# Attention of the even mixer regrouped from 32 steps of one head to 16 steps of two, and a small buffer padded

## The chip, the cores and the metric

The kernel runs on one core of a Trainium2 chip. The metric is the device time of one execution in microseconds; the time of a kernel is the median of its runs. A run that is profiled also leaves a trace of every instruction. TensorE (PE, with its weight loads as PEld), VectorE (DVE), ScalarE (ACT), GpSimd (POOL) and SyncE (SP) each work through a program of their own and meet at semaphores.

## What is computed

Two layers over 256 latent and 256 context tokens of width 1024, in float32. Each layer is a half-step FFN, a token mixer, a half-step FFN. The change lies in the mixer of the even layer, whose attention part is:

```python
s_band = jnp.einsum("bnqkgd,bnjkd->bkgnqj", qb, kb).astype(jnp.float32) * scale   # latent keys, |i-j| <= 128
s_ctx = jnp.einsum("bnqkgd,bckd->bkgnqc", qb, kc).astype(jnp.float32) * scale     # all context keys
p = jax.nn.softmax(jnp.concatenate([s_band, s_ctx, sink_logits(sink, s_band.shape)], axis=-1), axis=-1)
o = p[latent] @ v + p[context] @ vc
```

There are 8 query heads of 64 channels and 2 key heads. Latent queries see 512 keys, context queries the 256 context keys. A learned value per head, the sink, joins the softmax's sum. Beside the attention the same mixer has a convolution of 31 taps over 512 channels, and the adaLN parameters of later sub-layers (`silu(c) @ mod_w`) are computed while it runs.

## The kernel before, in words

**Order of the work.** Each engine has a hand-written program in one block. An FFN is a loop over "units": a unit's weights (up to 1 MB) come by DMA into `raw`, ACT rounds them into `w_hi` (L805), DVE makes the rest `w_lo` (L1083), and PE does three products per tile (`three`, L396 to L398): hi by hi, hi by lo, lo by hi. The up projection reads `hn_hi` and `hn_lo` as the moving operand, the down projection `a_hi` and `a_lo` (12 or 10 tiles of 512 tokens per unit, 8 units per half FFN). The last FFN has 256 tokens only.

**The even mixer** goes through 7 input units. PE does the first five whole; the two gate and value units of the convolution's last two channel groups are cut into 16 pieces (`conv_step`, six matmuls each), of which four go before the attention and 12 into it.

**The attention before.** `ATT` lists 32 steps (pair of heads tt, stream s, head of the pair h2, half of the queries qt). s = 0 is latent (512 keys), s = 1 context (256 keys). One step j goes through:
- PE `scores` (L570): the 128 queries by the keys, 64 channels deep, into bank 4 + j % 2. Head h2 sits on partitions 64·h2 to 64·h2 + 63, so on its own half of the array's rows. A float32 product is two passes, "x2" in the rows.
- DVE `largest`: mask and maximum (L1309) for s = 0, maximum (L1312) for s = 1, then the shift (L1314).
- ACT `expo`: the exponential with its sum (L926) and the sink's (L928).
- DVE `denominator` (L1321, L1322), ACT `normalise` (L934).
- PE `turn` (L579): 4 or 2 transposes into bank 6 + j % 2; ACT `turned` (L941) copies them to `pT`.
- PE `values` (L596): the product with V, 64 columns wide, in two halves spread over two steps; the group of four steps of one (tt, s) fills half of the partitions with each head. ACT `att_head` (L947) and DVE (L1333) then make `hn_hi` and `hn_lo` of it.

**The engines' loops** run one step after another, staggered: in round j PE issues `scores(j+1)`, conv pieces, `turn(j-1)`, `values` of an earlier step, and from round 10 on one quarter of an adaLN job (`mod_products`, L432: 8 products on 32 columns each, sixteen passes). DVE in round j does `largest(j)`, `denominator(j-1)`, the group's rest, and some taps of the convolution (`taps`, L1266, one tap for 128 channels and 512 tokens). ACT does `expo(j)`, `normalise(j-1)`, `turned(j-2)`. In rounds 4 and 9 ACT also makes a sigmoid (L961, its own table) and rounds a unit (L805), and DVE waits for the sigmoid (`gated_value`, L1252). All queues are in order.

**The adaLN jobs** 6 to 11 have 24 quarters of 1 MB each. `mod_raw` holds four; POOL issues the load (L388) of the next job's quarter as soon as PE has used the present one. After a job's four quarters ACT copies the row (`mod_rows`, L838), PE spreads it (`mod_columns`, L441, with `sel` as moving operand), DVE adds the bias (`mod_vector`, L1172). The first quarter of a job waits for the row of the job before.

**After the attention** PE sums the convolution's output over channels (L626), the layer norm follows (L1351 and others), and the output projection starts with the attention's half, then the convolution's.

**Memory.** On-chip buffers lie one behind the other in the order of their declaration, each rounded up to 32 bytes. `hn_hi` starts at byte 32896 of a partition (a multiple of 128). `sel` takes 32 bytes; behind it come `shared`, `c_act`, `modT`, then `a_hi`, `a_lo`, `mod_raw`, and in the same room the mixers' own buffers. `a_hi` starts at 146720, which is 32 past a multiple of 128. Weights (`w_hi`, `w_lo`) lie ahead of `sel`, on multiples of 128.

Of the kernel before, what the change touches and what calls it, by code (L numbers as in the profile page):

```python
# [84 lines left out]
def build(nc, t, out):  # L85
# [3 lines left out]
    with ExitStack() as ctx:  # L89
# [24 lines left out]
        sel = sb("sel", [P, 8])  # L114
# [90 lines left out]
        s_mm = sem("s_mm")  # L205
        max_made = sem("max_made")
# [65 lines left out]
        def att_slot(j):  # L272

            i = j - ATT_FROM
            return ATT_JOBS[0] + i // 4, i % 4
# [116 lines left out]
        def _(pe):  # L392
# [171 lines left out]
            def scores(j):  # L564
                tt, s, h2, qt = ATT[j]
                if j >= 2:
                    pe.wait_ge(exp_made, j - 1)
                k0 = LAT * s
                a = LAT * s + qt * P
                pe.matmul(ps[:, 4 + j % 2, k0:KEYS], qk[64 * h2:64 * h2 + 64, tt, a:a + P],  # L570
                          qk[64 * h2:64 * h2 + 64, CT, k0:KEYS], start=True, stop=True).then_inc(s_mm, 1)

            def turn(j):
                tt, s, h2, qt = ATT[j]
                pe.wait_ge(p_made, j + 1)
                if j >= 2:
                    pe.wait_ge(pT_made, j - 1)
                for kt in range(2 * s, 4):
                    last = pe.transpose(ps[:, 6 + j % 2, kt * P:(kt + 1) * P], prod[:, j % 2, kt * P:(kt + 1) * P],  # L579
                                        ident)  # L580
                last.then_inc(pT_mm, 1)

            def values(j, half):

                tt, s, h2, qt = ATT[j]
                g = j // 4
                kts = range(2 * s, 4)
                kts = kts[:len(kts) // 2] if half == 0 else kts[len(kts) // 2:]
                if half == 0:
                    pe.wait_ge(pT_made, j + 1)  # L590
                    if g >= 2:
                        pe.wait_ge(mix_made, g - 1)
                    if g == 0:
                        pe.wait_ge(unit_evac, E + 5)
                for kt in kts:
                    last = pe.matmul(ps[64 * h2:64 * h2 + 64, g % 2, 0:LAT], v_att[:, kt, 64 * h2:64 * h2 + 64],  # L596
                                     pT[:, (j // 2) % 2, kt, :], start=(kt == 2 * s), stop=(kt == 3))
                if half == 1:
                    last.then_inc(pv_mm, 1)

            NJ = len(ATT)
            scores(0)
            for j in range(NJ + 3):
                if j + 1 < NJ:
                    scores(j + 1)
                if j < 4:
                    conv_step(2, 4 + j)
                if 5 <= j < 9:
                    conv_step(3, 2 * j - 10)
                    conv_step(3, 2 * j - 9)  # L610
                if 1 <= j < NJ + 1:
                    turn(j - 1)
                if j >= 3:
                    values(j - 2 - (j + 1) % 2, (j + 1) % 2)
                if ATT_FROM <= j < ATT_FROM + 4 * len(ATT_JOBS):
                    m, q = att_slot(j)
                    mod_products(m, q, q + 1)
                    if q == 1 and m > ATT_JOBS[0]:
                        mod_columns(m - 1)
            mod_columns(ATT_JOBS[-1])  # L620
# [169 lines left out]
        def _(act):  # L790
# [128 lines left out]
            def expo(j):  # L919
                tt, s, h2, qt = ATT[j]  # L920
                act.wait_ge(max_made, j + 1)
                if j >= 2:
                    act.wait_ge(pT_mm, j - 1)
                src = ps[:, 4 + j % 2, LAT:KEYS] if s else gact[:, j % 2, :]
                neg = att_cols[:, 1, j:j + 1]
                act.activation(prod[:, j % 2, LAT * s:KEYS], src, ACT.Exp, bias=neg, scale=HD ** -0.5,  # L926
                               accum_out=att_cols[:, 2, j:j + 1])
                act.activation(att_cols[:, 3, j:j + 1], col("sink", tt + 4 * h2), ACT.Exp, bias=neg).then_inc(exp_made, 1)  # L928

            def normalise(j):  # L930
                tt, s, h2, qt = ATT[j]
                act.wait_ge(den_made, j + 1)
                p = prod[:, j % 2, LAT * s:KEYS]
                act.activation(p, p, ACT.Copy, scale=att_cols[:, 5, j:j + 1]).then_inc(p_made, 1)  # L934

            def turned(j):
                tt, s, h2, qt = ATT[j]
                act.wait_ge(pT_mm, j + 1)
                if j // 2 >= 2:
                    act.wait_ge(pv_mm, j // 2 - 1)  # L940
                act.activation(pT[:, (j // 2) % 2, 2 * s:4, qt * P:(qt + 1) * P],  # L941
                               ps[:, 6 + j % 2, 2 * s * P:4 * P].rearrange("p (k q) -> p k q", q=P),
                               ACT.Copy).then_inc(pT_made, 1)
# [767 lines left out]
```

## Time and profile before

| what | value |
|---|---|
| median of 3 runs | 1949.94 us (1946.14 to 1950.98) |
| the profiled execution's own time | 1950.95 us |
| its span | 1949.2 us |
| mean granted TensorE clock | 0.971 |
| PE / PEld / DVE / ACT busy | 95% / 77% / 46% / 32% |

The span is 1.75 us shorter than the execution's own time, which is 1.0 us above the median. PE is busy in nearly all of it. The attention stands between 508 and 641 us.

### The profile page before, as it was taken

What the parts mean: (1) busy time and instruction counts of PE and PEld (TensorE: products, weight loads), DVE (VectorE), ACT (ScalarE), POOL (GpSimd) and SP (SyncE); (2) the same over time, 40 slices, a digit from 0 to 9 for tenths busy, and PEclk for the clock granted to TensorE, in tenths of its full rate; (3) what the DMA queues carried; (4) which work ended last, traced back from release to release, by engine and by line L of the source; (5) the groups of instructions that cost most, each with busy time, mean ns of one, the idle gap of its engine ahead of it and who ended that gap; (6) DMA issues with size and microseconds to landing.
All of it is one profiled execution on the core that took longest, in us unless ns stands there. A gap on an engine that the chain in (4) does not pass through costs nothing.

```text
span 1949.2 us, 25181 instructions
## 1 busy us (share of the span) xinstructions
PE 1844.9 (95%) x10094; PEld 1491.5 (77%) x10094; DVE 887.5 (46%) x1375; ACT 614.6 (32%) x824; POOL 36.3 (2%) x72
## 2 busy tenths in 40 slices
PE   3999999999889999999999999999998998899996
PEld 1788778868544668888888688888877988589996
DVE  2433323345878552333334533333344455865555
ACT  2322122233445332212222322222223133244342
POOL 0000000000001000000000000000000000000000
PEclk7999999999899989999999999999998999999998
DMA  8522452243148353222213422232232224045553
GB/s 337 218 86 87 173 194 86 75 164 124 44 163 306 137 193 131 82 96 103 106 64 111 169 90 92 81 108 108 68 126 111 87 88 151 1 176 186 179 178 103
DMA packets 39108, 252.39 MB, mean 129 GB/s; under 512 B 4465, under 2 KB 5873, under 8 KB 14449
## 3 DMA queue, kind: packets, MB, share of 16 engines
q1 hardware_dynamic: 29232, 179.91, 26.3%
q0 software_dynamic: 9792, 71.31, 9.5%
q8 instruction: 61, 1.00, 0.2%
q14 instruction: 23, 0.18, 0.0%
HBM read 250.15 MB, written 1.05 MB: 129 GB/s over the span
## 4 chain that ended last, share of the span: by engine, by line
PE 87%; DVE 7%; ACT 2%; DMA 2%; issue 2%; SPq 0%; ACTq 0%; DVEq 0%
PE ps L396 26%; PE ps L398 26%; PE ps L397 26%; PE ps L432 3%; PE ps L596 1%; DMA xT<-in_xT 1%; DVE w_lo L1083 1%; DVE y L1266 1%; PE ps L570 1%; PE ps L743 1%; ACT w_hi L805 1%; PE ps L456 1%; PE ps L579 1%; DVE t_ring L1144 1%; PE ps L710 0%
## 5 line engine op out<-in xcount | busy, mean ns | idle before, releaser
L396 PE MATMUL ps<-hn_hi,w_hi 128*128 128x512 f32 (+2 forms) x1784 | 646.3, 362 | 12.4 <-DVE hn_lo L1160 8.2
L397 PE MATMUL ps<-hn_lo,w_hi 128*128 128x512 f32 (+2 forms) x1784 | 640.4, 359 | 0.0
L398 PE MATMUL ps<-hn_hi,w_lo 128*128 128x512 f32 (+2 forms) x1784 | 640.1, 359 | 0.0
L1083 DVE TENSOR_TENSOR w_lo<-raw,w_hi 128x2048 fp32r<-128x2048 f32 (+2 forms) x184 | 377.0, 2049 | 569.7 <-ACT w_hi L805 569.6
L805 ACT ACTIVATE w_hi<-raw 128x2048 fp32r<-128x2048 f32 (+2 forms) x184 | 316.6, 1721 | 823.5 <-PE ps L398 814.2
L396 PEld LDWEIGHTS ps<-hn_hi,w_hi 128*128 128x128 f32 (+1 forms) x1784 | 338.8, 190 | 77.3 <-issue 24.4
L398 PEld LDWEIGHTS ps<-hn_hi,w_lo 128*128 128x128 f32 (+1 forms) x1784 | 338.9, 190 | 50.5 <-issue 0.3
L397 PEld LDWEIGHTS ps<-hn_lo,w_hi 128*128 128x128 f32 (+1 forms) x1784 | 339.1, 190 | 48.4 <-issue 0.7
L396 PE MATMUL ps<-a_hi,w_hi 128*128 128x512 f32 (+1 forms) x704 | 258.9, 368 | 1.8 <-DVE a_lo L1198 1.8
L398 PE MATMUL ps<-a_hi,w_lo 128*128 128x512 f32 (+1 forms) x704 | 258.5, 367 | 0.0
L397 PE MATMUL ps<-a_lo,w_hi 128*128 128x512 f32 (+1 forms) x704 | 258.5, 367 | 0.0
L1101 DVE SCALAR_TENSOR_TENSOR xT<-ps,modT,xT 128x256 f32 (+1 forms) x136 | 59.9, 479 | 235.3 <-PE ps L398 235.3
L396 PEld LDWEIGHTS ps<-a_hi,w_hi 128*128 128x128 f32 x704 | 132.5, 188 | 26.8 <-DVE a_lo L1198 2.2
L398 PEld LDWEIGHTS ps<-a_hi,w_lo 128*128 128x128 f32 x704 | 132.5, 188 | 24.2
L397 PEld LDWEIGHTS ps<-a_lo,w_hi 128*128 128x128 f32 x704 | 132.5, 188 | 24.1
L863 ACT ACTIVATE a_hi<-prod 128x512 f32 (+3 forms) x88 | 50.9, 578 | 212.3 <-DVE prod L1195 212.3
L432 PE MATMUL ps<-mod_raw,c_act 128*32 128x256 f32 x1152 | 84.6, 430 | 17.5 <-DMA mod_raw<-in_mod_w 13.8
L1198 DVE TENSOR_TENSOR a_lo<-prod,a_hi 128x512 f32 (+3 forms) x88 | 55.1, 626 | 71.7 <-ACT a_hi L863 71.7
L432 PEld LDWEIGHTS ps<-mod_raw,c_act 128*32 128x32 f32 x1152 | 34.8, 119 | 62.0 <-issue 36.7
L1266 DVE SCALAR_TENSOR_TENSOR y<-upad,cols,y 128x512 f32<-128x512 f32 x120 | 82.0, 743 | 0.0
L396 PE MATMUL ps<-w_hi,hn_hi 128*128 128x256 f32 x256 | 76.1, 297 | 4.9 <-DVE shared L1394 4.9
L397 PE MATMUL ps<-w_lo,hn_hi 128*128 128x256 f32 x256 | 73.7, 288 | 0.0
(181 smaller groups left out, 1182.6 us busy)
## 6 DMA issues: line engine op xcount, KB each, us to landing
raw<-in_w_up SPq DMA_DIRECT2D x88, 1024.0 KB, 4.9
mod_raw<-in_mod_w POOLq DMA_DIRECT2D x68, 1024.0 KB, 7.1
raw<-in_w_downA SPq DMA_DIRECT2D x32, 768.0 KB, 4.3
raw<-in_w_downB SPq DMA_DIRECT2D x32, 640.0 KB, 3.9
raw<-in_w_od_in SPq DMA_DIRECT2D x16, 1024.0 KB, 4.8
raw<-in_w_ev_in SPq DMA_DIRECT2D x7, 1024.0 KB, 4.9
mod_raw<-in_mod_w SPq DMA_DIRECT2D x4, 1024.0 KB, 11.0
raw<-in_w_ev_out SPq DMA_DIRECT2D x4, 1024.0 KB, 4.9
```

The source lines that it names most:

```text
L396: pe.matmul(o, lh, rh, start=first, stop=False)
L397: pe.matmul(o, lh, rl, start=False, stop=False)
L398: return pe.matmul(o, ll, rh, start=False, stop=last)
L432: last = pe.matmul(ps[32 * g:32 * g + 32, product_bank(m), 0:LAT], c_act[:, k, :], mod_raw[:, k, g * LAT:(g + 1) * LAT], start=(k == 0), s ...
L456: pe.matmul(ps[:, 7, 0:W[n]], ones, rstd[:, 0:W[n]], start=True, stop=True).then_inc(rstd_mm, 1)
L570: pe.matmul(ps[:, 4 + j % 2, k0:KEYS], qk[64 * h2:64 * h2 + 64, tt, a:a + P], qk[64 * h2:64 * h2 + 64, CT, k0:KEYS], start=True, stop=True ...
L805: act.activation(w_hi[:, u0 % 2, 0:n], raw[:, u0 % 2, 0:n], ACT.Copy).then_inc(hi_made, 1)
L863: act.activation(a_hi[:, j + 2 * r, 0:w], prod[:, j, 0:w], ACT.Copy).then_inc(a_hi_made, 1)
L1083: dve.tensor_tensor(w_lo[:, u0 % 2, 0:n], raw[:, u0 % 2, 0:n], w_hi[:, u0 % 2, 0:n], ALU.subtract).then_inc(lo_made, 1)
L1101: last = dve.scalar_tensor_tensor(out=xT[:, d0 + 2 * r, tokens(s)], in0=ps[:, bank(u0, b), tokens(s)], scalar=modT[:, vec, d0 + 2 * r, s:s ...
L1198: dve.tensor_tensor(a_lo[:, j + 2 * r, 0:w], prod[:, j, 0:w], a_hi[:, j + 2 * r, 0:w], ALU.subtract).then_inc(a_made, 1)
L1266: ins = dve.scalar_tensor_tensor(out=dst, in0=src, scalar=col("conv_w", i * CT + c), in1=dst, op0=ALU.mult, op1=ALU.add)
```

## The change

There are 16 steps now: `ATT` is (tt, qt, s), and a step holds both heads of a pair. The stream s alternates from step to step. The two heads' score products are issued one behind the other: for s = 0 into banks 4 and 5, for s = 1 into the two halves of bank 1, where the second waits for the first (`s_half`) and a conv piece or an adaLN quarter stands between. Transposes go to banks 6 and 7, one for each head. The value products of both heads alternate, all into bank 0. DVE and ACT handle two heads per operation where they can. The conv pieces stand in rounds 0 to 8 (`CONV_AT`), two adaLN quarters go into each of the rounds 10 to 21, and the loops run to round 22 or 23. `sel` is padded to 32 floats.

```diff
-        sel = sb("sel", [P, 8])
+        sel = sb("sel", [P, 32])[:, 0:8]
-            pT = sb("pT", [P, 2, 4, LAT], F32, s)
+            pT_full = sb("pT_full", [P, 2, 4, LAT], F32, s)
+            pT_ctx = sb("pT_ctx", [P, 2, 2, LAT], F32, s)
+        def att_quarters(j):
+            at = [2 * (j - ATT_FROM) + i for i in range(2)]
+            return [(ATT_JOBS[0] + i // 4, i % 4) for i in at if 0 <= i < 4 * len(ATT_JOBS)]
+        def att_rows(j):
+            return [m for i, m in enumerate(ATT_JOBS) if j == ATT_FROM + 2 * i + 2]
+        CONV_AT = {0: ((2, 4), (2, 5)), 1: ((2, 6),), 2: ((2, 7),), 4: ((3, 0),), 5: ((3, 1), (3, 2)),
+                   6: ((3, 3), (3, 4)), 7: ((3, 5), (3, 6)), 8: ((3, 7),)}
+        GATED_AT = {3: 2, 9: 3}
-        EARLY = 28
+        EARLY = 30
         def taps_by(j):
             if j < 9:
-                return EARLY + (TAPS - EARLY) * (j + 1 if j < 4 else j) // 8
-            return min(2 * TAPS, TAPS + TAPS * (j - 9) // 24)
+                return EARLY + (TAPS - EARLY) * (j + 1) // 9
+            return min(2 * TAPS, TAPS + TAPS * (j - 8) // 12)
-        ATT = [(tt, s, h2, qt) for tt in range(4) for s in range(2) for h2 in range(2) for qt in range(2)]
+        ATT = [(tt, s, qt) for tt in range(4) for qt in range(2) for s in range(2)]
@@ PE
+            def score(j, h2):
+                tt, s, qt = ATT[j]
+                if h2 == 0 and j >= 2:
+                    pe.wait_ge(exp_made, j - 1)
+                if h2 == 1 and s == 1:
+                    pe.wait_ge(s_half, j // 2 + 1)
...
+                last = pe.matmul(score_place(s)[:, h2, :], qk[64 * h2:64 * h2 + 64, tt, a:a + P],
+                                 qk[64 * h2:64 * h2 + 64, CT, LAT * s:KEYS], start=True, stop=True)
+            def values(tt, s):
+                g = 2 * tt + s
+                pe.wait_ge(pT_made, 4 * tt + 2 + s + 1)
+                if g >= 1:
+                    pe.wait_ge(mix_made, g)
...
+                for i, kt in enumerate(att_keys(s)):
+                    for h2 in range(2):
+                        last = pe.matmul(ps[64 * h2:64 * h2 + 64, 0, 0:LAT], v_att[:, kt, 64 * h2:64 * h2 + 64],
+                                         turned_place(s)[:, h2, i, :], start=(i == 0), stop=(kt == 3))
+            for j in range(NJ + 7):
+                between = [(conv_step, a) for a in CONV_AT.get(j, ())]
+                between += [(mod_products, (m, q, q + 1)) for m, q in att_quarters(j)]
                 if j + 1 < NJ:
-                    scores(j + 1)
+                    score(j + 1, 0)
+                    if ATT[j + 1][1] == 1:
+                        step, a = between.pop(0)
+                        step(*a)
+                    score(j + 1, 1)
+                for step, a in between:
+                    step(*a)
                 if 1 <= j < NJ + 1:
                     turn(j - 1)
+                if j >= 5 and (j - 5) % 4 < 2 and j < NJ + 3:
+                    values((j - 5) // 4, (j - 5) % 4)
+                for m in att_rows(j):
+                    mod_columns(m)
@@ ACT
+                for h2 in range(2):
+                    i = 2 * j + h2
+                    src = gact[:, h2, :] if s == 0 else score_place(s)[:, h2, :]
+                    act.activation(weight_place(s)[:, h2, :], src, ACT.Exp, bias=att_cols[:, 1, i:i + 1],
+                                   scale=HD ** -0.5, accum_out=att_cols[:, 2, i:i + 1])
...
+                act.activation(turned_place(s)[:, :, :, qt * P:(qt + 1) * P],
+                               ps[:, 6:8, 0:n * P].rearrange("p h (k q) -> p h k q", q=P), ACT.Copy).then_inc(pT_made, 1)
+                if j in GATED_AT:
...
+                if j >= 6 and (j - 6) % 4 < 2 and j < NJ + 4:
+                    att_head(2 * ((j - 6) // 4) + (j - 6) % 4)
@@ DVE
                 if s == 0:
+                    for h2 in range(2):
+                        last = dve.tensor_tensor_reduce(out=gact[:, h2, :], in0=score_place(s)[:, h2, :],
+                                                        in1=att_mask[:, qt, :], scale=1.0, scalar=-3e38, op0=ALU.add,
+                                                        op1=ALU.max, accum_out=top[:, h2:h2 + 1])
                 else:
+                    link(dve.reduce_max(top, score_place(s), AX.X))
+                dve.scalar_tensor_tensor(out=att_cols[:, 1, 2 * j:2 * j + 2], in0=top, scalar=-HD ** -0.5, in1=sinks,
+                                         op0=ALU.mult, op1=ALU.min).then_inc(max_made, 1)
-                if j >= 7 and (j - 3) % 4 == 0:
+                if j >= 7 and (j - 7) % 4 < 2 and j < NJ + 5:
+                    g = 2 * ((j - 7) // 4) + (j - 7) % 4
-                if j in (11, 13):
-                    rest_of(E + 7 + (j - 11) // 2)
+                if j in (10, 11):
+                    rest_of(E + 7 + j - 10)
+                for m in att_rows(j - 1):
+                    mod_vector(m)
```

## Rows read from the trace of the kernel before

**Rows 1.** The page: busy time of the engines, share of the span, instructions.
```profile
PE 1844.9 (95%) x10094; PEld 1491.5 (77%) x10094; DVE 887.5 (46%) x1375; ACT 614.6 (32%) x824; POOL 36.3 (2%) x72
```
**Rows 2.** Chain that ended last, 400 to 1000 us: start, us, what.
```profile
509.12 2.65 DVE y L1266 x4
...
560.91 2.20 DVE w_lo L1083
...
641.29 3.54 PE ps L626 x8
```
**Rows 3.** Busy time by stretch; last three: granted clock, DMA share, GB/s.
```profile
526.00:534.00 8.00, 7.93 (x22) 5.07 (x21) 5.74 (x15) 6.77 (x10) 0.00 (x0) 0.57 0.00 0
571.00:641.00 70.00, 65.51 (x519) 29.61 (x515) 56.28 (x147) 35.49 (x105) 11.64 (x22) 1.00 0.91 316
```
**Rows 4.** Waits, 507 to 645 us: total, times, longest.
```profile
DVE hn_lo L1333 <- ACT hn_hi L947: 12.1, 8, 3.7
...
DVE upad L1252 <- ACT t_ring L961: 7.4, 2, 3.9
```
**Rows 5.** PE in order of time: start, us, instructions with their count.
```profile
586.34 0.65 PE L596 MATMUL ps<-pT,v_att 128*64 128x256 f32 x2
586.91 1.07 PE L432 MATMUL ps<-mod_raw,c_act 128*32 128x256 f32 x16
587.91 1.12 PE L570 MATMUL ps<-qk 64*128 64x512 f32 x2
588.97 0.66 PE L579 MATMUL ps<-mats,prod 128*128 128x128 f32 x4
...
596.92 1.08 PE L596 MATMUL ps<-pT,v_att 128*64 128x256 f32 x4
...
598.93 0.70 PE L570 MATMUL ps<-qk 64*128 64x256 f32 x2
```
**Rows 6.** DVE in order of time: an s = 0 round, then an s = 1 round.
```profile
515.45 0.68 DVE L1309 CUSTOM_DVE_ANT_0 gact<-ps,att_mask 128x512 f32<-128x512 f32 x1
...
516.57 2.72 DVE L1266 SCALAR_TENSOR_TENSOR y<-upad,cols,y 128x512 f32<-128x512 f32 x4
...
532.21 0.42 DVE L1312 TENSOR_REDUCE att_cols<-ps 128x1 f32<-128x256 f32 x1
...
533.06 2.72 DVE L1266 SCALAR_TENSOR_TENSOR y<-upad,cols,y 128x512 f32<-128x512 f32 x4
```
**Rows 7.** ACT in order of time, round 4 with its sigmoid.
```profile
524.98 0.71 ACT L934 ACTIVATE prod<-prod,att_cols 128x512 f32<-128x512 f32 x1
525.59 0.58 ACT L941 ACTIVATE pT<-ps 128x512 f32<-128x512 f32 x1
526.19 1.28 ACT L961 ACT_TABLE_LOAD   x1
527.49 0.60 ACT L961 ACTIVATE t_ring<-ps 128x512 f32<-128x512 f32 x1
...
531.20 0.48 ACT L926 ACTIVATE prod<-ps,att_cols 128x256 f32<-128x256 f32 x1
```
**Rows 8.** Landing times of `mod_raw` 440 to 650 us; two stretches of the DMA.
```profile
DMA to landing us min/median/max: 5.0/5.3/8.0
...
435.00:445.00 10.00, 8.87 (x40) 6.05 (x40) 9.21 (x23) 5.50 (x13) 0.53 (x1) 0.67 1.01 425
636.00:640.00 4.00, 3.93 (x40) 1.41 (x38) 2.11 (x5) 0.41 (x2) 1.09 (x3) 1.00 0.94 360
```
**Rows 9.** Matmul groups of the first FFN (60 to 425 us), then of the last.
```profile
L397 PE MATMUL ps<-hn_lo,w_hi 128*128 128x512 f32 x339 | 131.9, 389 | 0.0
L397 PE MATMUL ps<-a_lo,w_hi 128*128 128x512 f32 x174 | 69.0, 396 | 0.0
...
L397 PE MATMUL ps<-hn_lo,w_hi 128*128 128x256 f32 x416 | 118.0, 284 | 0.0
L397 PE MATMUL ps<-a_lo,w_hi 128*128 128x256 f32 x176 | 49.2, 280 | 0.0
```

More of the change, by code:

```diff
@@ L562, in _ @@
             pe.wait_ge(v_made, 1)
-            def scores(j):
-                tt, s, h2, qt = ATT[j]
-                if j >= 2:
+            def score(j, h2):
+                tt, s, qt = ATT[j]
+                if h2 == 0 and j >= 2:
                     pe.wait_ge(exp_made, j - 1)
-                k0 = LAT * s
+                if h2 == 1 and s == 1:
+                    pe.wait_ge(s_half, j // 2 + 1)
                 a = LAT * s + qt * P
-                pe.matmul(ps[:, 4 + j % 2, k0:KEYS], qk[64 * h2:64 * h2 + 64, tt, a:a + P],
-                          qk[64 * h2:64 * h2 + 64, CT, k0:KEYS], start=True, stop=True).then_inc(s_mm, 1)
+                last = pe.matmul(score_place(s)[:, h2, :], qk[64 * h2:64 * h2 + 64, tt, a:a + P],
+                                 qk[64 * h2:64 * h2 + 64, CT, LAT * s:KEYS], start=True, stop=True)
+                if h2 == 1:
+                    last.then_inc(s_mm, 1)
+                elif s == 1:
+                    last.then_inc(s_half, 1)
@@ L573, in turn @@
             def turn(j):
-                tt, s, h2, qt = ATT[j]
+                tt, s, qt = ATT[j]
                 pe.wait_ge(p_made, j + 1)
[L576 to L580, printed above, removed]
-                last.then_inc(pT_mm, 1)
[L583 to L599, printed above, removed]
@@ L601, in _ @@
-            NJ = len(ATT)
-            scores(0)
-            for j in range(NJ + 3):
-                if j + 1 < NJ:
-                    scores(j + 1)
[L606 to L610, printed above, removed]
+                if j >= 1:
+                    pe.wait_ge(pT_made, j)
+                for h2 in range(2):
+                    for i in range(len(att_keys(s))):
+                        last = pe.transpose(ps[:, 6 + h2, i * P:(i + 1) * P],
+                                            weight_place(s)[:, h2, i * P:(i + 1) * P], ident)
@@ new lines, in turn @@
+                last.then_inc(pT_mm, 1)
+            def values(tt, s):
[3 more added lines that the diff above has]
+                    pe.wait_ge(mix_made, g)
+                else:
+                    pe.wait_ge(unit_evac, E + 5)
+                for i, kt in enumerate(att_keys(s)):
+                    for h2 in range(2):
+                        last = pe.matmul(ps[64 * h2:64 * h2 + 64, 0, 0:LAT], v_att[:, kt, 64 * h2:64 * h2 + 64],
+                                         turned_place(s)[:, h2, i, :], start=(i == 0), stop=(kt == 3))
+                last.then_inc(pv_mm, 1)
@@ L930, in normalise @@
+                for h2 in range(2):
+                    i = 2 * j + h2
+                    last = act.activation(att_cols[:, 3, i:i + 1], col("sink", tt + 4 * h2), ACT.Exp,
+                                          bias=att_cols[:, 1, i:i + 1])
+                last.then_inc(exp_made, 1)
             def normalise(j):
-                tt, s, h2, qt = ATT[j]
+                tt, s, qt = ATT[j]
                 act.wait_ge(den_made, j + 1)
-                p = prod[:, j % 2, LAT * s:KEYS]
-                act.activation(p, p, ACT.Copy, scale=att_cols[:, 5, j:j + 1]).then_inc(p_made, 1)
+                for h2 in range(2):
+                    p = weight_place(s)[:, h2, :]
+                    last = act.activation(p, p, ACT.Copy, scale=att_cols[:, 5, 2 * j + h2:2 * j + h2 + 1])
@@ L936, in turned @@
+                last.then_inc(p_made, 1)
             def turned(j):
-                tt, s, h2, qt = ATT[j]
+                tt, s, qt = ATT[j]
+                n = len(att_keys(s))
                 act.wait_ge(pT_mm, j + 1)
[L939 to L943, printed above, removed]
+                if tt >= 1 and qt == 0:
+                    act.wait_ge(pv_mm, 2 * (tt - 1) + s + 1)
@@ L945, in att_head @@
+                act.activation(turned_place(s)[:, :, :, qt * P:(qt + 1) * P],
+                               ps[:, 6:8, 0:n * P].rearrange("p h (k q) -> p h k q", q=P), ACT.Copy).then_inc(pT_made, 1)
             def att_head(g):
[L946 to L947 removed]
+                act.wait_ge(pv_mm, g + 1)
+                act.activation(hn_hi[:, CT + g // 2, tokens(g % 2)], ps[:, 0, 0:LAT], ACT.Copy).then_inc(att_hi, 1)
@@ L949, in _ @@
             NJ = len(ATT)
-            for j in range(NJ + 3):
+            for j in range(NJ + 7):
+                for m in att_rows(j):
+                    mod_rows(m)
                 if j < NJ:
@@ L956, in _ @@
                     turned(j - 2)
-                if j in (4, 9):
-                    c = 2 if j == 4 else 3
+                if j in GATED_AT:
+                    c = GATED_AT[j]
                     act.wait_ge(unit_mm, E + 4 + c)
```

66 lines of the change are left out of this document (24 added, 42 removed).

## The prediction, made before the changed kernel was run

> **What bounds the kernel now.** I began with the page: PE is busy for 95% of the span [rows 1], and the FFNs around the mixer keep it so. Where a stage lasts as long as PE's instructions, only fewer or shorter PE instructions help. Next the chain of waits: in the attention it first runs through DVE's taps, then through PE, and at 641.29 it enters the sum for the layer norm [rows 2]. DVE's first softmax part ends in taps at 509.12, so the stage runs from 508 to 641.3, some 133 us. The busy time by stretch shows two halves. From 571 to 641 PE is busy for 65.5 of 70 us at the full clock, and the DMA engines for 91% [rows 3]. Before that the engines wait for each other, and the clock was granted at 0.57 in one stretch, that is, mostly at 1.2 instead of 2.4 GHz [rows 3]. The waits tell for what: DVE stood 7.4 us before the two sigmoids and 12.1 us before the eight head outputs [rows 4].
>
> **PE's terms.** Taken at the full clock, start to start (a row's length less some 0.07 that it overlaps the next) [rows 5]: a 512-key score 1.06 us (two passes of about 0.43 and 0.2 of filling after another shape), a 256-key score 0.63; four transposes 0.59 (0.11 each and 0.15 per call; one pass of 128 columns is half of a 256-column pass); two value passes 0.57, four 1.00 (0.22 each, 0.15 per call); an adaLN quarter 1.00.
> Do two products side by side share their time? The quarter shows it: its sixteen passes of 256 columns take 1.00 us, four take 1.00 us in the value products [rows 5]. Four column strips ran at once. I take this for two column halves (values) and, less surely, for two row halves (scores); no row shows the latter. Bounds for a pair of 512-key scores: 1.1 (together) to 1.9 (in turn); I take 1.1.
> - Scores: before 16·1.06 + 16·0.63 = 27; after 8·1.1 + 16·0.63 = 19, as the 256-key ones stay apart. Minus 8, at worst minus 1.
> - Values: 96 passes in 32 calls were 16·1.00 + 16·0.57 = 25; after, 96·0.22/2 + 8·0.15 = 12. Minus 13, at worst minus 3.
> - Transposes: same 96, half the calls: minus 16·0.15 = 2.4.
> - Conv pieces, quarters and `mod_columns` stay.
> PE had some 112 us of work at the full clock and keeps about 88. It will no longer be the bound, so these 24 us are not the gain.
>
> **DVE's terms.** An s = 0 round takes 1.12 us before its taps (515.45 to 516.57), an s = 1 round 0.85 (532.21 to 533.06) [rows 6]; a tap 0.66 (four in 2.65 [rows 2]). A two-head round repeats the 0.61 mask operation and its reading of the sum: 1.8 us. With s = 1 the maximum covers 512 instead of 256 numbers, plus 0.27: 1.12 us. So 16·(1.12 + 0.85) = 31.5 becomes 8·(1.8 + 1.12) = 23.4.
>
> **ACT's stall.** DVE waits for each sigmoid, behind what ACT has queued. In the new rounds 3 and 9 (both s = 1) these are two exponentials (0.36 + 0.10 each) and two sink terms (0.18 each), 1.3; normalising two 512-wide heads, 1.24; a 512-wide copy, 0.58 (round 3: two heads of 256); the table 1.28 and the sigmoid 0.6 [rows 7]. Together 5.0, less 0.2 of DVE work beside it: 4.8, twice, where the two took 7.4 before [rows 4]. PE runs dry there too, its clock falls, and it catches up at half speed while DVE still has taps; I count that at nothing as long as DVE is behind.
>
> **Sum of the stage.** DVE from round 0 to the end of round 15: 68 taps, 44.6; softmax parts, 23.4; five head outputs, 1.7; two units' rests of 2.2 [rows 2], 4.4; the two gated values, 1.2; two `mod_vector`, 0.3; stalls, 9.6. That is 85.2 us, so round 16 begins at 508.2 + 85.2 = 593.4. PE in these rounds has 37 + 33 = 70, ACT some 60. The 12.1 us before head outputs shrink to little: each output now has a whole round between its steps. Bound: 0 to 12; I take 0, with the range for the rest.
> From round 16 on there is no softmax. DVE has 26 taps and little else, 19 us. But 12 quarters are left, two per round, and the DMA has to bring eight of them after their room is freed: the first is asked for at 1.6 us into round 16, lands after 5.3 us (median [rows 8]), and seven follow at the rate of a full queue, 425 GB/s, 1.049 MB in 2.47 us [rows 8]. The last lands at 593.4 + 1.6 + 5.3 + 17.3 = 617.6. Its products, row and columns add 2.1: 619.7. The PE idles in this tail, and I add 2 us for some of it and of the layer norm's sum at 1.2 GHz (bounds 0 and 6). The norm's sum then starts at 621.5 instead of 641.3: **minus 19.8 us**. What follows is unchanged.
>
> **The padding.** `sel` grows from 32 to 128 bytes, so all behind it moves by 96, and `a_hi` from 32 past a multiple of 128 to a multiple of 128. Does PE read it faster? In the first FFN a 512-wide matmul with `a_lo` moving takes 396 ns, with `hn_lo`, which lies on such a multiple, 389 [rows 9]. Weights, clock and width are the same. The other difference is that the down projection adds into one bank without alternating; but with 256 tokens, where that would hurt more, `a_lo` is the faster one, 280 against 284 [rows 9]. This leaves the address as the likelier cause, though why only the long stream would pay for it no row tells. The 512-wide down projections have 3·8·22·3 = 1584 such matmuls, back to back and on the chain. At 7 ns each: **minus 11.1 us**. Bounds: plus 2 (the 528 short ones lose their 4 ns) and minus 16 (it falls to the short ones' overhead, 10 ns less). The mixer's buffers move too; no row prices that, nothing is taken.
>
> **Total.** 1950.95 − 19.8 − 11.1 = 1920.1 for an execution like the profiled one; the median was 1.0 lower, so **1919**.
>
> **The rivals.**
> 1. **The address does nothing** and one bank without alternation is what costs 7 ns. For it: nothing else in the kernel has 512-wide products into one bank, so the rows cannot part the two. Then 1949.94 − 19.8 = 1930. Chance 0.30.
> 2. **No sharing of time.** The two halves of the array work in turn. PE then needs 8·0.8 + 10 = 16 us more, 43 instead of 37 in rounds 0 to 8, where DVE has 41, and 40 of 44 in 9 to 15. About 5 us are lost: 1924. The quarters [rows 5] speak against it for columns. Chance 0.06.
> 3. **The DMA is slower in the tail.** With fewer loads in flight it moved 360 GB/s near 640 us [rows 8]; then a quarter takes 2.91 us and eight cost 3.5 us more: 1923. Chance 0.07. The Trainium skill, "DMA: Bandwidth & Descriptors" (Specifications), gives about 358 GB/s from HBM per core where both cores of the memory stream. By it this rival would hold, with the same 1923; the 425 GB/s of the first row speak against it, taken while this core alone ran the kernel.
> 4. **Slower than before: the round trip.** PE is in order, and `values(tt, 1)` in rounds 6, 10, 14 and 18 waits for `mix_made`, which DVE gives in its next round, behind `largest` and `denominator`, which need PE's scores and ACT's exponentials. Likewise `turn(j-1)` waits for ACT's queue with the next step's exponentials ahead. If PE stands there before it has issued the next score, nothing overlaps and a step costs the whole trip: score 1.1, maximum 1.8, exponentials 1.8, sum 0.2, normalising 1.2, transposes 1.0, copy 1.0, and 2.4 to 3.4 of taps in between, 11 us. It decides from 7.5 us per step: 16·7.5 + 23 equals the old 133 and the padding's gain. At 11 us the stage takes 199 − 10 for overlap of the ends, 56 more, or some 1995 with the padding. Against it: the score of step j + 1 is issued ahead of that wait in each case, so a trip has 4.1 to 6 us of slack. Chance 0.05.
> 5. **The clock stays low** through the tail and into the output projection: 10 us of dense matmuls at half speed, 5 to 8 more: 1926. Chance 0.07.
> The forecast keeps 0.45.
>
> **How the numbers follow.** The forecast's own spread is ±6 (0 to −6 for the clock, head outputs, bounds of the padding). The range 1911 to 1936 takes in rivals 1, 2, 3 and 5; outside lie rival 4 and tails, under 0.2. A change of less than 0.3%, 5.8 us, is about what a measurement of this kernel cannot tell from none. Slower are rival 4 (0.05) and 0.02 of rival 1's 0.30, for waits that eat more than the stage's 20 us; another 0.04 of rival 1 is a stage that gives back 14 us or more: no difference. So 0.89, 0.04 and 0.07.
>
> **What the profile after would show.** If right: L626 starts near 621 (and 3.7 earlier if the padding works, as a third of its matmuls lie in the first FFN: near 618); in the rounds to 15 the chain runs through DVE's taps with PE idle in each; two DVE waits of 4 to 5 us before L1252; in the tail PE waits for DMA `mod_raw`; score pairs start within a few ns; `a_lo` matmuls take 389. Wrong: `a_lo` still at 396 (rival 1), values at 0.22 per pass (rival 2), PE waiting on DVE L1333 in each group (rival 4), PEclk 0.5 after 620 (rival 5).

## The result, and the profile after

The changed kernel takes **1935.93 us** (median of 6 runs, 1930.73 to 1940.88), the kernel before 1950.88 (6 runs, 1946.14 to 1951.27). The ratio is 0.9924, with an interval of 0.9907 to 0.9941: faster by some 15 us, where 31 were forecast. The time lies inside the stated range, 0.1 us from its upper end; the gain is half of the one forecast. The profiled execution took 1935.99 us, with a span of 1934.2 and a mean granted clock of 0.967.

I read the views in the order of the prediction. The padding first: the matmul groups of the first FFN (60 to 420 us), then those with 256 tokens; columns are busy us, mean ns of one, idle.

```profile
L422 PE MATMUL ps<-hn_lo,w_hi 128*128 128x512 f32 x336 | 130.7, 389 | 0.0
L422 PE MATMUL ps<-a_lo,w_hi 128*128 128x512 f32 x175 | 68.1, 389 | 0.0
...
L422 PE MATMUL ps<-hn_lo,w_hi 128*128 128x256 f32 x544 | 154.6, 284 | 0.0
L422 PE MATMUL ps<-a_lo,w_hi 128*128 128x256 f32 x176 | 49.8, 283 | 0.0
```

Against [rows 9] `a_lo` fell from 396 to 389 ns with 512 columns, and rose from 280 to 283 with 256. `hn_lo`, whose buffer did not move, is where it was. So this term came as forecast.

Then PE's work in the attention, in order of time, from 583 us on.

```profile
583.78 1.13 PE L596 MATMUL ps<-qk 64*128 64x512 f32 x4
...
587.91 1.95 PE L624 MATMUL ps<-pT_full,v_att 128*64 128x256 f32 x16
...
594.47 1.08 PE L624 MATMUL ps<-pT_ctx,v_att 128*64 128x256 f32 x8 [0.78 <-DVE hn_lo L1370]
```

Both kinds of pairs (scores on two halves of the array's rows, values on two halves of its columns) share their time. Four score passes of 512 columns take what two took before (1.12 us in [rows 5]), and sixteen value passes 1.88 us (1.95 less the overlap), where four took 1.00. That too is as forecast.

The gain is missing in the time of the stage. From DVE's first mask operation (502.54 us; 508.18 before) to the layer norm's sum it lasts 129.7 us; it was 133.1, and 113.3 was forecast. The chain of waits (start, us, what; from three of its windows) tells where:

```profile
520.05 0.61 ACT t_ring L998
520.68 0.69 DVE upad L1286
...
530.30 2.01 PE ps L596 x4
532.31 0.73 PE ps L421
...
559.09 0.61 ACT t_ring L998
559.72 0.70 DVE upad L1286
...
598.29 8.56 DMA mod_raw<-in_mod_w
...
609.16 7.61 DMA mod_raw<-in_mod_w
...
618.21 11.25 DMA mod_raw<-in_mod_w
...
632.25 3.54 PE ps L654 x8
```

It no longer runs through DVE's taps alone. Twice it comes from a sigmoid; behind the first a score pair takes 2.01 us for 1.06, and conv pieces at half clock follow. (I call a stretch cold when the clock is granted at about 0.5 in it.) At the end it goes three times through a transfer: 27.4 of the last 34 us. The waits between 500 and 640 us (total, times, longest):

```profile
DVE modT L1206 <- PE ps L466: 12.1, 2, 6.2
DVE upad L1286 <- ACT t_ring L998: 11.5, 2, 5.9
PE ps L457 <- DMA mod_raw<-in_mod_w: 9.7, 8, 3.0
PE ps L610 <- ACT pT_full L977: 9.7, 5, 3.9
PE ps L610 <- ACT pT_ctx L977: 4.5, 2, 2.3
DVE att_cols L1349 <- PE ps L596: 8.3, 3, 6.1
DVE hn_lo L1370 <- ACT hn_hi L982: 3.5, 1, 3.5
```

`modT` and `hn_lo` are waits of the tail, where DVE has nothing else to do. `upad` is the gate, 11.5 us where the prediction had 9.6. `att_cols` is a wait of DVE for scores: 0.2 us in round 3, 6.1 in round 7 and 1.9 in round 9, which the prediction did not expect. The two rows of L610 are PE's transposes, which stood 14.2 us, in seven waits, before ACT's copies. The longest of them comes behind the first sigmoid:

```profile
529.21 1.09 PE L610 MATMUL ps<-mats,sq 128*128 128x128 f32 x4 [3.93 <-ACT pT_full L977]
```

The two kernels' text tells why. Before, `turn` waited for ACT's copy of the step two back, as the transposes alternated between banks 6 and 7; now each step fills both banks, and `turn(j-1)` waits for the copy of the step just before it, which in ACT's round stands behind `expo(j)` and `normalise(j-1)`. The kernel before has no such wait in this stretch; its transposes stood 8.8 us, in four waits, before ACT's normalised rows. Neither the prediction nor an experiment is about this, and no run gives the second pair of banks back. Busy time by stretch (the last three: granted clock, DMA share, GB/s):

```profile
526.00:534.00 8.00, 4.79 (x12) 2.69 (x13) 6.90 (x18) 6.16 (x18) 0.00 (x0) 0.64 0.00 0
571.00:641.00 70.00, 57.13 (x516) 30.23 (x517) 48.61 (x98) 24.03 (x62) 11.66 (x22) 0.87 0.93 365
580.00:632.00 52.00, 40.29 (x428) 20.33 (x418) 36.38 (x73) 18.05 (x47) 10.60 (x20) 0.87 1.00 401
```

PE is no longer full (57 of 70 us, 65.5 in [rows 3]), and DVE less so. The DMA is what is full: 100% for 52 us. The landing times of `mod_raw` from 560 to 650 us:

```profile
DMA to landing us min/median/max: 5.1/8.2/11.2
```

They were 5.0/5.3/8.0 in [rows 8]. And from POOL in order of time the requests that open and close the prediction's tail, the 13th (round 16) and the 20th (the last that the stage needs):

```profile
600.32 0.53 POOL L413 DMA_DIRECT2D mod_raw<-in_mod_w  x1 [1.49 <-PE ps L457]
...
618.21 0.53 POOL L413 DMA_DIRECT2D mod_raw<-in_mod_w  x1 [1.53 <-PE ps L457]
```

These two requests cut the stage into the prediction's two sums. **Part A**, from the first mask operation to the 13th request, was forecast at 86.8 us (593.4 + 1.6 − 508.2) and took 97.8. **Part B**, from there to the norm's sum, was forecast at 26.5 and took 31.9. All later figures of A and B are read in the same way, each from the one profiled execution of its kernel. How far such a figure can be trusted, four kernels show whose program is the same up to the 13th request but for addresses or the size of the loads: the changed kernel, e2, e3 and e4 have parts A of 97.8, 99.9, 97.8 and 98.9 us.

### The profile page after: what moved, and what is told of

Read it like the earlier page. It is cut to its first block, busy times and chain, and to the rows that moved or that the text cites. A ratio compares the mean times of both kernels' runs of the same rounds, so it can differ in the third digit from the quotient of the medians.

```text
span 1934.2 us, 25050 instructions
## 1 busy us (share of the span) xinstructions
PE 1814.2 (94%) x10094; PEld 1488.0 (77%) x10094; DVE 878.0 (45%) x1319; ACT 613.0 (32%) x808; POOL 36.4 (2%) x72
## 4 chain that ended last, share of the span: by engine, by line
PE 84%; DVE 9%; DMA 3%; ACT 3%; issue 1%; SPq 0%; ACTq 0%; DVEq 0%
PE ps L421 26%; PE ps L422 26%; PE ps L423 26%; DVE y L1300 2%; PE ps L457 2%; DMA mod_raw<-in_mod_w 1%; DVE w_lo L1117 1%; DMA xT<-in_xT 1%; DVE t_ring L1178 1%; PE ps L771 1%; DVE hn_lo L1194 1%; ACT w_hi L833 1%; PE ps L481 1%; PE ps L738 0%; DVE acc L1130 0%
```

## The experiments

The first four runs are about two theories: the padding and the regrouping each alone (e1, e2), and the queue in the tail, taken down in two ways (e3, e4).

**e1_pad_only**, the kernel before with the buffer padded:

```diff
-        sel = sb("sel", [P, 8])
+        sel = sb("sel", [P, 32])[:, 0:8]
```

> The kernel before with sel padded to 32 floats and nothing else. Address theory: the 1584 512-wide matmuls that read a_hi and a_lo fall from 396 to 389 ns (minus 11.6 us at the pitch of 234 to 227 ns), the 528 256-wide ones rise from 280 to 283 (plus 1.8 us), so 1950.9 becomes 1941, ratio 0.995; the attention still takes 133 us. Rival, the shorter matmuls come with the new order of the attention: a_lo stays at 396 and the time at 1951.

Measured: 1938.59 us (5 runs), ratio 0.9937 (0.9923 to 0.995). Its first FFN:

```profile
L397 PE MATMUL ps<-hn_lo,w_hi 128*128 128x512 f32 x336 | 130.8, 389 | 0.0
L397 PE MATMUL ps<-a_lo,w_hi 128*128 128x512 f32 x176 | 68.5, 389 | 0.0
```

The down projection still adds into one bank without alternating, and takes 389 ns. Only addresses moved, so rival 1 falls, and the padding is worth 12.2 us, by the interval of the ratio between 10 and 15. Its stage takes 132.1 us, 1.0 less than before.

**e2_no_pad**, the changed kernel with `sel` as before:

```diff
-        sel = sb("sel", [P, 32])[:, 0:8]
+        sel = sb("sel", [P, 8])
```

> The changed kernel with sel back at 8 floats: the attention part alone. Address theory: a_lo at 396 again, 1935.9 becomes 1946, and against the kernel before 4 to 5 us are left, since the stage took 129.7 us against 133.1. Rival, the address also matters inside the attention (its buffers moved by the same 96 bytes): the stage from the first mask operation to the sum for the layer norm is longer than 129.7 by over 2 us.

Measured: 1947.42 us (11 runs), ratio 0.9982 (0.9971 to 0.9992), and the slow reading is back:

```profile
L422 PE MATMUL ps<-hn_lo,w_hi 128*128 128x512 f32 x337 | 131.2, 389 | 0.0
L422 PE MATMUL ps<-a_lo,w_hi 128*128 128x512 f32 x169 | 67.0, 396 | 0.0
```

The regrouping alone is worth 3.4 us, by the interval between 1.6 and 5.7. 12.2 and 3.4 make 15.6, the whole gain within what the runs can tell.

**e3_half_loads**, the changed kernel in which jobs 7 to 11 load half of each quarter:

```diff
-                    pool.dma_start(mod_raw[:, 2 * q:2 * q + 2], t["mod_w"][m][:, 2 * q:2 * q + 2]).then_inc(mod_in[q], 16)
+                    n = 1 if 7 <= m <= 11 else 2
+                    pool.dma_start(mod_raw[:, 2 * q:2 * q + n], t["mod_w"][m][:, 2 * q:2 * q + n]).then_inc(mod_in[q], 16)
```

> The changed kernel in which the 20 quarters of the adaLN jobs 7 to 11 load 512 KB instead of 1 MB; the second half of each keeps what the job before left there, so these adaLN parameters are not the reference's. Theory, the DMA sets the tail: its queue was full from 580 to 632 us, now 10 MB less have to come at some 410 GB/s, the waits of 8.6, 7.6 and 11.3 us for mod_raw vanish, DVE's taps end the stage near 621 instead of 632, so about 11 us are gained: 1925. Rival, the tail is held by PE at its lower clock and by the row, column, vector steps of each job: under 3 us are gained.

Measured: 1925.17 us (4 runs), ratio 0.9865 (0.985 to 0.988), 10.8 us under the changed kernel. Its stretch, and the norm's sum in its chain:

```profile
580.00:632.00 52.00, 46.37 (x466) 26.33 (x466) 40.52 (x81) 20.17 (x51) 10.55 (x20) 0.97 0.75 262
```

```profile
621.33 5.23 PE ps L655 x8
```

The queue is busy for 75% instead of 100%. Part A is 97.8 us, the same as with full loads; part B falls from 31.9 to 20.1. So the queue costs nothing in rounds 0 to 15 that these profiles could show, and 12 us behind them. Of these, 1.7 are lost again at once, as the norm's sum runs at half clock (5.23 us for 3.54).

**e4_five_jobs**, job 11 moved out of the attention, behind it:

```diff
-        UP_JOB = {"f0A": 2, "f0B": 4, "f1A": 13}
-        DOWN_JOB = {"f0A": 3}
-        NORM_JOB = {1: 5, 2: 12, 3: 14, 4: 15, 5: 17}
-        ATT_JOBS = range(6, 12)
+        UP_JOB = {"f0A": 2, "f0B": 4, "f1A": 12}
+        DOWN_JOB = {"f0A": 3, "f1A": 13}
+        NORM_JOB = {1: 5, 2: 11, 3: 14, 4: 15, 5: 17}
+        ATT_JOBS = range(6, 11)
```

> The changed kernel with the adaLN job 11 taken out of the attention: the jobs 11, 12 and 13 move one place on (norm 2, then the up and the down projection of the first half of FFN f1). DMA theory: 4 quarters, 4.2 MB, less in the tail at 400 GB/s shorten it by 10.4 us, down to the end of the taps; the job costs 3.6 + 0.4 us of PE time in the FFN instead: 6 to 7 us faster than the changed kernel, 1929 to 1930. Rival, the tail isn't the DMA's: 4 us slower than the changed kernel, 1940.

Measured: 1928.79 us (4 runs), ratio 0.9878 (0.9861 to 0.9894), with nothing left out, 7.1 us under the changed kernel. The sum starts at 620.25 us, 12 earlier, and what follows is 5.6 us longer in the span (1307.6 for 1302.0): some 1.5 of it the sum at half clock, 5.01 us for 3.54; the other 4.1 are close to the 4.0 that was expected for the job in its new place. Part B is 18.7 us, with four transfers in it instead of eight.

The next four are about part A: ACT's order (e5, e6), the clock (e7), and ACT's order in both ways together with five jobs (e8).

**e5_ring**, the changed kernel with ACT's round in another order:

```diff
-                if j < NJ:
-                    expo(j)
                 if 1 <= j < NJ + 1:
                     normalise(j - 1)
                 if 2 <= j < NJ + 2:
                     turned(j - 2)
+                if j < NJ:
+                    expo(j)
```

> Changed kernel with ScalarE's order in a round turned round: normalise(j-1), turned(j-2), then expo(j), where the change has expo(j) first. If the ring of waits between ScalarE and TensorE (expo(j) waits for turn(j-2), the normalise of the round before queues behind it; 7.3 us in 'ACT prod waits for PE ps', 5.9 in 'ACT sq waits for PE ps') slows the rounds, it goes, and the time falls by 3 to 6 us, to 1930 to 1933. If the rounds are set by the stalls at the gated sigmoid and by the DMA tail alone, the time stays within 1.5 us of 1936. If expo being later makes the transposes of P late, VectorE waits longer for the scores and it is slower by 2 to 5 us (1938 to 1941).

Measured: 1935.2 us (5 runs), ratio 0.9926 (0.9912 to 0.9939). Part A is 97.5 us. PE's waits for ACT's copies fell from 14.2 to 9.0 us, DVE's for scores from 8.3 to 7.3, and two short waits of DVE for ACT, 2.9 us together, came in their place. Alone the order does nothing that can be measured.

**e6_sigmoid_first**:

```diff
+                if j in GATED_AT:
+                    c = GATED_AT[j]
+                    act.wait_ge(unit_mm, E + 4 + c)
+                    act.activation(t_ring[:, c % 2, :], ps[:, 3, :], ACT.Sigmoid).then_inc(gate_made, 1)
                 if j < NJ:
                     expo(j)
...
                 if j in GATED_AT:
-                    c = GATED_AT[j]
-                    act.wait_ge(unit_mm, E + 4 + c)
-                    act.activation(t_ring[:, c % 2, :], ps[:, 3, :], ACT.Sigmoid).then_inc(gate_made, 1)
                     head_of(E + 5 + c)
```

> Changed kernel with the gated sigmoid (and its table load) first in ScalarE's rounds 3 and 9, ahead of the exponentials instead of behind them. Theory: VectorE stands 5.9 and 5.6 us at the product with the gate in those two rounds (before: 4.8 and 2.6 or so), because its own round has become shorter and the sigmoid comes last; with the sigmoid first the two waits together shrink from 11.5 us to 3 to 6, the start of round 16 moves up by 5 to 8 us, and the time falls by 4 to 8, to 1928 to 1932. Rival (the tail is set by the queue of transfers and any gain ahead of it is lost there): the two waits shrink, the queue of the five jobs starts as late as before, and the time stays within 1.5 us of 1936. A second rival: the exponentials come later by the table loads, VectorE does not need the gate earlier but TensorE's transposes wait, and the stall only moves to the scores of rounds 5 to 7: same time.

Measured: 1933.19 us (5 runs, 1925.94 to 1936.62), ratio 0.99 (0.9883 to 0.9918), 2.7 under the changed kernel, less than the 4 that were expected at least, and hardly clear of nothing, as the two intervals overlap. (Of the two waits before the change, which the expectation puts at 4.8 and 2.6 us, the trace of before has 3.55 and 3.86.) Its waits:

```profile
DVE att_cols L1350 <- PE ps L596: 12.7, 6, 4.6
...
DVE upad L1287 <- ACT t_ring L992: 3.6, 2, 2.0
```

The gate's wait fell by 7.9 us, and the one for scores rose by 4.4. At the gate of round 9 DVE was 7.7 us ahead (49.5 us after its first mask operation for 57.2), at the 13th request 2.9 (A is 94.9), and at the norm's sum 3.5; the sum itself then ran at half clock, 6.21 us for 3.54. The wait for scores came already in round 5, 4.6 us long, where the changed kernel has none: this is the expectation's second rival. Between 577 and 584 us PE, after it had stood 2.3 us before ACT's copy, ran cold (32 adaLN products in 3.10 us for 1.93). The queue was full too, with 389 GB/s from 580 to 632 us. So it isn't the queue alone that takes the gain, as the first rival had it.

**e7_warm**, the changed kernel with matmuls of no use in PE's idle time behind the first sigmoid:

```diff
+                if j in (3, 4):
+                    for i in range(8 if j == 3 else 16):
+                        pe.matmul(ps[:, 0, :], hn_hi[:, 0, 0:P], hn_hi[:, 0, :], start=True, stop=True)
                 if 1 <= j < NJ + 1:
                     turn(j - 1)
```

> Changed kernel with filler matmuls that compute nothing used (8 of 128x512 in round 3, 16 in round 4, into a bank that is free there), in the idle time of TensorE behind the stall at the sigmoid. Theory: TensorE idles 2.3 and 3.9 us there, its clock is then granted 0.5 from 528 to 535 us, the convolution pieces and scores behind run at half speed, and VectorE waits 6.1 us for the scores of round 7. With the clock kept at 1.0 that wait shrinks by 2 to 5 us and the time falls by as much, to 1931 to 1934. If the wait at round 7 comes from the order of work and not from the clock, it stays above 5 us and the time is within 1 us of 1936, or 1 to 3 us longer for the fillers.

Measured: 1934.15 us (5 runs), ratio 0.9909 (0.9894 to 0.9924), 1.8 under the changed kernel, which these runs can't part from nothing. The profile shows what the fillers did to the clock in that stretch, and to DVE's wait in round 7:

```profile
526.00:534.00 8.00, 6.40 (x32) 4.36 (x31) 7.86 (x20) 6.02 (x18) 0.00 (x0) 1.00 0.00 0
```

```profile
539.35 0.69 DVE L1352 TENSOR_REDUCE att_cols<-ps 128x2 f32<-128x512 f32 x1 [4.46 <-PE ps L596]
```

The clock stayed at 1.00, the wait in round 7 was 4.46 us, where the changed kernel has 6.12 and e2, e3 and e4 have 5.13, 6.16 and 5.14, and part A took 95.6 us, 2.2 less. That is about as much as the parts A of those like kernels differ. So the cold clock can be a small part of that wait, and most of it stays at full clock. I put it down to PE being late from the sigmoid on, which no run shows by itself.

**e8_combined**, with the tables of e4 and this order of ACT's round: the sigmoid if `j in GATED_AT`, `normalise(j - 1)`, `turned(j - 2)`, `expo(j)`, `head_of`.

> Job 11 moved out of the attention (1928.8 in its own run, 7 under the changed kernel), ScalarE's order of e5 and the sigmoid first in rounds 3 and 9. If the losses in rounds 0 to 15 and in the tail lie one behind the other they add: 7 + 3 to 6 + 4 to 8 under 1936, 1915 to 1922. If the ring and the stall are the same idle time counted twice, one of the two is lost: 1921 to 1925. If gains ahead of the tail are taken back by the queue: 1927 to 1930.

Measured: 1921.53 us (4 runs, 1915.75 to 1924.09), ratio 0.9853 (0.9838 to 0.9868), 7.3 us under e4. Its waits, and the norm's sum in its chain:

```profile
DVE att_cols L1350 <- PE ps L596: 7.1, 4, 2.9
...
DVE upad L1287 <- ACT t_ring L992: 2.3, 2, 1.5
```

```profile
610.94 3.54 PE ps L654 x8
```

The stage takes 105.9 us from the first mask operation (505.04) to that sum.

The last four ask: is the stage before bound by the queue too (e9), and does the reordering pay when the queue is out of the way (e10)? Then two variants of e8.

**e9_before_half**: e1 with the edit of e3.

> Kernel before with the padded buffer, and jobs 7 to 11 load only half of each quarter (512 KB for 1 MB): their modulation parameters are then not the reference's. With e1 (the same with full loads, 1938.6) and the pair of the changed kernel (1935.9 with full loads, 1925.2 with half) this is a square. Theory: before, VectorE's 24 taps and scores fill the stage and the queue is not what ends it; half loads change it by at most 3 us, to 1935 to 1939, and the sharing is worth 10 to 13 us when the loads are halved, against 3 with full loads. Rival: the queue was the bound of the stage before too; then half loads give it 6 us or more, 1932 or less, and the sharing's worth does not depend on the loads.

Measured: 1936.58 us (5 runs), ratio 0.9931 (0.9917 to 0.9946). The queue is no bound of the stage before: 2.0 us under e1, which the intervals can't part from nothing, its stage 133.1 us as before. With halved loads the regrouping is worth 1936.58 − 1925.17 = 11.4 us, with full loads 2.7.

**e10_half_reordered**: e3 with ACT's order of e8.

> Changed kernel with the half loads of e3 (1925.2; jobs 7 to 11 load half, so their parameters are not the reference's) and ScalarE's order of e8: sigmoid first in rounds 3 and 9, normalise and turned ahead of expo. In e6 VectorE was 7 us earlier at round 9 and the stage ended at the same time, as the queue had taken it back. Theory: with the queue out of the way the 7 us come through: 1916 to 1919, and the stage takes 110 to 113 us, near the 113.3 of the prediction. Rival: the gain at round 9 is lost in the rounds behind for another reason (order of work, clock), and it stays at 1923 to 1926.

Measured: 1915.7 us (5 runs), ratio 0.9829 (0.9812 to 0.9845). Its stage takes 111.2 us (A 89.9, B 21.3). The 13th request on POOL, and the norm's sum in the chain:

```profile
592.42 0.53 POOL L414 DMA_DIRECT2D mod_raw<-in_mod_w  x1 [1.50 <-PE ps L458]
```

```profile
613.75 5.17 PE ps L655 x8
```

Against e9 that is a gain of 20.9 us for regrouping and order together, close to the 19.8 that the prediction gave to the regrouping alone. The nearness is in part chance: A is still 3.1 us longer than forecast, and B, with half the bytes, 5.2 shorter than a forecast made for all of them. But the two places where gain was lost show in it: 8.8 us (10.8 less the 2.0 that e9 gains too) come back when the queue is relieved, and 9.5 more when ACT's order is changed, sigmoid and `expo` together.

**e11_five_sigmoid**: e4 with e6's edit, so `expo` stays ahead of `normalise`.

> Job 11 moved out of the attention and the sigmoid first in rounds 3 and 9, with expo ahead of normalise and turned as in the changed kernel (e8 without the other order of ScalarE's round). If that order is worth nothing, as its own run e5 says (1935.2 against 1935.9), 1921 to 1923 as e8. If the ring of waits between ScalarE and TensorE only shows once the two longer stalls are gone, it is 2 to 4 us above e8: 1924 to 1926.

Measured: 1921.51 us (4 runs, 1920.42 to 1926.21), ratio 0.9854 (0.9838 to 0.9869), the same as e8. Its part A is 94.9 us.

**e12_five_all**: e8 with the fillers of e7.

> e8 with the filler matmuls of e7 in rounds 3 and 4. In e8 VectorE still waits 2.1 and 2.9 us for the scores behind round 4 with the clock partly low. If these come from the clock, 1 to 3 us below e8: 1919 to 1921. If the queue of transfers (e8 has it full from 560 to 615 us) takes gains ahead of it back, the same as e8 within 1 us; if the fillers now stand in TensorE's way, 1 to 2 us above.

Measured: 1923.93 us (4 runs, 1921.96 to 1927.67), ratio 0.9867 (0.9852 to 0.9882). That is a miss: no gain, and by the medians 2.4 us above e8, which the intervals can't part from nothing. It is no test of a warm clock either, as the clock fell all the same: the 16 fillers of round 4 took 6.11 us, where e7's took 3.92. Behind them the scores came late for a mask operation of DVE:

```profile
534.27 0.69 DVE L1348 CUSTOM_DVE_ANT_0 gact<-ps,att_mask 128x512 f32<-128x512 f32 x1 [3.19 <-PE ps L596]
```

So here the fillers stood in PE's way, as the last of the three expectations had it. Part A is 94.3 us.

| kernel | median us | A | B |
|---|---|---|---|
| forecast | 1919 | 86.8 | 26.5 |
| changed | 1935.9 | 97.8 | 31.9 |
| e2, no padding | 1947.4 | 99.9 | 29.0 |
| e3, half loads | 1925.2 | 97.8 | 20.1 |
| e4, five jobs | 1928.8 | 98.9 | 18.7 |
| e5, `expo` last | 1935.2 | 97.5 | 30.8 |
| e6, sigmoid first | 1933.2 | 94.9 | 31.3 |
| e7, fillers | 1934.2 | 95.6 | 29.4 |
| e10, half loads and order | 1915.7 | 89.9 | 21.3 |
| e11, five jobs, sigmoid first | 1921.5 | 94.9 | 19.2 |
| e8, five jobs and order | 1921.5 | 87.3 | 18.6 |
| e12, e8 with fillers | 1923.9 | 94.3 | 19.1 |

In e4, e8, e11 and e12 part B has four transfers instead of eight. The profiled execution of e8 was the fastest of its four, those of e3 and e6 were the slowest of theirs, so the 7.6 us between the parts A of e8 and e11 stand against no difference at all in the medians. Whether the order of `normalise` and `expo` gives anything once the sigmoid is first stays open.

## Why the prediction was right, and where it was wrong

**Padding: right.** Forecast 11.1 us from 1584 matmuls of 7 ns; e1 gives 12.2. The argument from the 256-token rows, that the address is the likelier cause than the bank, held. The sum left out the 528 matmuls with 256 columns, which by the rows became 3 ns longer (1.6 us); the runs are too coarse to show that.

**Sharing on PE: right**, rows and columns both, and so was the reading that PE's 24 us are not the gain.

**The stage: wrong by 16.4 us**, 113.3 forecast and 129.7 taken. By the prediction's own steps:

1. Part A, 11.0 us too short. The step that failed is a cost put at nothing: "PE runs dry there too, its clock falls, and it catches up at half speed while DVE still has taps; I count that at nothing as long as DVE is behind." Behind the first sigmoid PE was late, partly cold, and DVE used up its taps and then waited 8.1 us for scores (8.3 with a short wait ahead of the sigmoid). Another 1.9 us are the two gate waits, priced at 4.8 us each and measured at 5.9 and 5.6, and 1.0 is a wait for the scores of a mask operation. That makes 11.2. By these waits a stall of DVE was counted once where it costs twice: the engines behind it restart late. e6 shows how the two hang together: its gate waits are 7.9 us shorter, and its part A only 2.9. In e10 A is shorter by 7.9. How much of PE's lateness is the stall, how much the cold clock and how much the transposes' wait for the copy of the step before stays open.

2. Part B, 5.4 us too short. The step that failed is the landing: "the first is asked for at 1.6 us into round 16, lands after 5.3 us (median [rows 8]), and seven follow at the rate of a full queue". The first took 9.0 us to land, 3.7 more than the term had. The seven behind it took 20.1 us, 2.87 each, where 2.47 (17.3 in all) was forecast: the queue was full, but it moved 390 GB/s between 606.85 and 629.46 us, not 425, and requests of the next job already shared it. The sum of the stage left these out. Together that is 6.5 us too little, against 1.1 too much for what follows the last landing (2.8 us for 3.9). The 5.3 us come from the stage before, where 24 requests went out between 561.89 and 639.68 us, one in 3.4 us, and the queue had room. In the changed kernel two go out in each round of 5 to 6 us, from round 12 on, so that the staging's four quarters are in flight together. Four times 2.47 us would make 9.9, an estimate from [rows 8]; the median was 8.2 and the last took 11.3. e3 and e9 show it from both sides: half the bytes shorten B by 12 us after the change, and leave the stage before as it was.

One slip of adding is in it too: 619.7 and 2 make 621.7, where the sum goes on with 621.5.

**The rivals.** 1 fell with e1 and e2, 2 with the rows of the pairs. 3 was near the truth: the queue did decide the tail, and its quarters landed 2.87 us apart, where rival 3 had 2.91. But it had no longer landing of the first one, and its reason, few loads in flight, is not what happened: four were in flight, and the queue moved 390 GB/s in that stretch and 401 over the 52 us, not 360. The Trainium skill, "DMA: Bandwidth & Descriptors" (Specifications), has about 358 GB/s per core where both share the memory. This core ran alone, so that limit does not speak of this case, and the measurement decides. 4 did not come as a whole: `values` waited 3.7 us in all for DVE's `hn_lo`. But what it says of `turn(j-1)`, that it waits for ACT's queue with the next step's exponentials ahead, fits PE's 14.2 us before the transposes. 5 came in part: the clock was at 0.53 between 620 and 631 us, while PE waited for transfers, but the sum ran at full clock (3.54 us).

**The range** held the time because it reached for rival 1, not because a case in it described what happened. The loss in part B was in sight: the DMA was at 91% in the second half before the change [rows 3], and a stage that is to be 20 us shorter with the same bytes needs more than that leaves.

**What beats both kernels**: e8 and e11, at 1921.5 us, 1.5% under before, by moving one job out and the sigmoid ahead. (e3 and e10 leave out half of the loads of five jobs, and do not compute what the reference does.)

## What to carry to other kernels

Before shortening a stage, divide the bytes that it must bring by its new length, and if the queue is then full, take the landing time with all staging in flight (buffers times bytes over the rate; 9.9 us by that estimate here, and 9.0 to 11.3 measured in the tail's first and last), not the median of the slack case. A removed load on the bound engine pays only until the next engine or queue that was at 90%; the square of two edits (e1, e9, changed, e3) shows this in four kernels. When two units of work are made one, look whether they also took both halves of a double buffer: here the transposes did, and PE stood 14.2 us before their copies. And look for a long operation that stands last in an engine's round although another engine waits for it: every round made shorter makes that wait longer.

## What the runs showed of the hardware that I had not expected

- The address of the moving operand matters: `a_lo` at 32 past a multiple of 128 bytes takes 396 ns per 128x512 matmul, on the multiple 389 (e1, e2). With 256 columns it is the other way, 280 and 283. Why is open.
- The clock's part was small where I looked for it: at 1.00 instead of 0.64 in the stretch from 526 to 534 us (e7), part A was 2.2 us shorter of 97.8, about as much as the parts A of kernels alike up to there differ. Fillers don't always hold it: in e12 the clock had fallen before those of round 4, and the 16 of them took 6.11 us for e7's 3.92.
- Executions of one program differ by more than many of these effects: 1930.7 to 1940.9 us for the changed kernel. The parts of a single profile are not a median.
